# Two unused buffers shift the addresses of all large buffers of a dense two-layer kernel

## The reference

```python
# first block
h = h + 0.5 * swiglu(rms_norm(h, ffn1_norm), w_gate, w_up, w_down)        # 1024 -> 2 x 2816 -> 1024
z = rms_norm(h, mix_norm) @ w_in                                           # all projections of the mixer
y_a = dsa_attention(...)                                                   # top-128 sparse attention
y_r = group_norm_heads(retention(rq, rk, rv), ret_gn) * silu(rg)
merged = sigmoid(ga) * (y_a @ w_branch_a) + sigmoid(gb) * (y_r @ w_branch_b)
h = h + merged @ w_out
h = h + 0.5 * swiglu(rms_norm(h, ffn2_norm), ...)
h = h + sigmoid(rms_norm(h, ple_norm) @ w_ple_gate) * (p @ w_ple_proj)
x = rms_norm(h, final_norm)
# second block
x = x + gla_mixer(rms_norm_2(x, l0_norm1), ...)                            # gated linear attention
x = x + conv_ffn(rms_norm_2(x, l0_norm2), ...)                             # conv of width 3, gated MLP
return rms_norm_2(x, final_norm_2)
```

## The kernel before

| buffer | first byte | modulo 256 |
|---|---|---|
| w_raw, w_hi, w_lo (L196 to L198) | 16512, 32896, 49280 | 128 |
| h, u_hi, u_lo | 65664, 82048, 98432 | 128 |
| tmp, side, ssum, rstd, ones | 114816 to 135296 | 128 |
| consts | 136864 | 160 |
| hid_hi, hid_lo (L227) | 138432, 183488 | 192 |
| yr, gy (hi and lo) | 138432, 154816 | 192 |
| mg (hi and lo) | 171200, 187584 | 192 |
| p_hi, p_lo | 199872, 203968 | 192 |
| ya_hi, ya_lo, behind `avt` of 1152 bytes | 210240, 218432 | 64 |

## Time and profile before

### The profile page before, as it was taken

One profiled execution on the slowest core, in us unless ns is written; L12 is line 12 of the kernel. 1 busy time (PEld: TensorE's weight loads), 2 busy tenths in 40 slices (PEclk: granted clock), 3 DMA queues, 4 the chain that ended last, 5 costly groups with the idle time before them and its releaser, 6 DMA issues.

```text
span 1906.7 us, 23739 instructions
## 1 busy us (share of the span) xinstructions
PE 1859.7 (98%) x8550; PEld 1497.7 (79%) x8550; DVE 798.5 (42%) x1266; ACT 707.6 (37%) x944; POOL 909.4 (48%) x708
## 2 busy tenths in 40 slices
PE   7999999999999889999999999999999999999998
PEld 5888888876888557878888888887877888888886
DVE  5222236216666545234222222256666465455212
ACT  6443423222333453234444322245325344444221
POOL 4544445386666414444444445343443454444542
PEclk9999999999999989999999999999999999999998
DMA  4323233242322212222332333232221232233331
GB/s 160 120 89 103 91 99 100 74 142 70 127 83 72 84 34 78 95 89 93 99 99 88 101 91 98 74 123 68 67 79 65 89 99 91 96 99 96 91 99 45
DMA packets 52530, 174.55 MB, mean 92 GB/s; under 512 B 6368, under 2 KB 6752, under 8 KB 52464
## 3 DMA queue, kind: packets, MB, share of 16 engines
q1 hardware_dynamic: 52288, 173.37, 28.4%
q10 hardware_dynamic: 176, 0.30, 0.1%
HBM read 166.56 MB, written 2.10 MB: 88 GB/s over the span
## 4 chain that ended last, share of the span: by engine, by line
PE 95%; DVE 2%; ACT 2%; DMA 1%; issue 0%; SPq 0%; DVEq 0%; ACTq 0%
PE acc L1483 28%; PE acc L1485 28%; PE acc L1484 28%; PE acc L1550 2%; PE acc L1552 2%; PE acc L1551 2%; PE aux L1676 1%; PE aux L1705 1%; ACT w_hi L632 1%; PE aux L1658 1%; PE acc L1729 1%; PE acc L1813 0%; PE acc L1808 0%; DVE probs L1225 0%; PE aux L1799 0%
## 5 line engine op out<-in xcount | busy, mean ns | idle before, releaser
L551 POOL TENSOR_TENSOR w_lo<-w_raw,w_hi 128x512 fp32r<-128x512 f32 (+1 forms) x633 | 822.5, 1322 | 960.3 <-ACT w_hi L632 960.2
L1483 PE MATMUL acc<-u_hi,w_lo 128*128 128x512 f32 x1592 | 632.3, 397 | 12.3 <-POOL w_lo L551 9.8
L1485 PE MATMUL acc<-u_hi,w_hi 128*128 128x512 f32 x1592 | 623.0, 391 | 0.0
L1484 PE MATMUL acc<-u_lo,w_hi 128*128 128x512 f32 x1592 | 623.0, 391 | 0.0
L632 ACT ACTIVATE w_hi<-w_raw 128x1024 fp32r<-128x1024 f32 (+1 forms) x317 | 326.6, 1034 | 569.9 <-PE acc L1485 510.0
L1483 PEld LDWEIGHTS acc<-u_hi,w_lo 128*128 128x128 f32 x1592 | 299.7, 188 | 89.1 <-issue 19.1
L1485 PEld LDWEIGHTS acc<-u_hi,w_hi 128*128 128x128 f32 x1592 | 299.6, 188 | 65.2
L1484 PEld LDWEIGHTS acc<-u_lo,w_hi 128*128 128x128 f32 x1592 | 299.9, 188 | 63.7 <-issue 2.0
L1483 PE MATMUL acc<-hid_hi,w_lo 128*128 128x512 f32 x528 | 208.0, 394 | 0.0
L1485 PE MATMUL acc<-hid_hi,w_hi 128*128 128x512 f32 x528 | 207.0, 392 | 0.0
L1484 PE MATMUL acc<-hid_lo,w_hi 128*128 128x512 f32 x528 | 204.9, 388 | 0.0
(11 more groups left out here) (286 smaller groups left out, 1977.7 us busy)
## 6 DMA issues: line engine op xcount, KB each, us to landing
w_raw<-in_w_up SPq DMA_DIRECT2D x132, 512.0 KB, 3.5
w_raw<-in_w_mix SPq DMA_DIRECT2D x69, 512.0 KB, 3.6
w_raw<-in_w_down SPq DMA_DIRECT2D x48, 512.0 KB, 3.5
w_raw<-in_w_gla SPq DMA_DIRECT2D x32, 512.0 KB, 3.4
w_raw<-in_w_down SPq DMA_DIRECT2D x24, 384.0 KB, 3.1
w_raw<-in_w_ple SPq DMA_DIRECT2D x10, 512.0 KB, 3.5
tmp<-tmp SPq DMA_DIRECT2D x36, 64.0 KB, 2.0
h<-in_xT SPq DMA_DIRECT2D x8, 256.0 KB, 7.1
```

The lines of the kernel that those rows point to most:

```text
L551: ins = pool.tensor_tensor(w_lo[:, slot, part], w_raw[:, slot, part], w_hi[:, slot, part].bitcast(F32), ALU.subtract)
L1483: pe.matmul(o, w_lo[:, slot, columns], x_hi, start=first, stop=False)
L1484: pe.matmul(o, w_hi[:, slot, columns], x_lo, start=False, stop=False)
L1485: return pe.matmul(o, w_hi[:, slot, columns], x_hi, start=False, stop=last)
```

## The change

A buffer of 8 float32 a partition is allocated ahead of `w_raw`, and one of 2 float32 ahead of the region. Nothing reads or writes them. No other line changes.

```diff
@@ -193,6 +193,7 @@
             return ctx.enter_context(nc.semaphore(name))
 
 
+        sb("pad_ring", [P, 8])
         w_raw = sb("w_raw", [P, RING, SLAB])
         w_hi = sb("w_hi", [P, RING, SLAB], F32R)
         w_lo = sb("w_lo", [P, RING, SLAB], F32R)
@@ -222,6 +223,8 @@
         ident = consts[:, C_ID:C_ID + P]
         gain_sq, tok_root = small[:, 40:48], small[:, 24:32]
 
+
+        sb("pad_region", [P, 2])
 
         with ExitStack() as region:
             hid_hi = sb("hid_hi", [P, KF, S], F32R, region)
```

## The result

The changed kernel takes 1916.91 us (median of 4 runs, 1916.03 to 1917.93), against 1905.42 us for the kernel before (4 runs): a ratio of 1.0055, 95% interval 1.0042 to 1.0068. It is slower by some 8 to 13 us.

The account below looks back on a forecast made before the run. TensorE, busy 98% of the span, was taken to bound the kernel. The terms sum to +2.4 us, all from the region's tiles, on a median of 1905.55, giving 1908.0 us; range 1898 to 1920, meant to hold 8 in 10.

Parts of the forecast that it names:

- The bound: Whole kernel: TensorE, busy 98% of the span, bounds it; the weight path runs ahead and is held back by it.
- Where the buffers go: SBUF addresses modulo 256: ring, h and u go from 128 to 160, hid and gy from 192 to 0, ya to 128.
- Part 1: 4728 u matmuls and 768 token matmuls: operands shift by 32 together, so 0 us; u bounds -63 to +32 us.
- Rival 3: Odd 32 bytes cost in ring and u: u goes to ya's price, +32 us, 1937.7 us; chance 0.10.
- Part 2: 2208 matmuls on hid, yr, gy, mg, p: 228.9 to 230.0 ns each, +2.4 us; bounds -4.9 to +10.2.
- the straight line through the prices at 0, 64 and 192: Matmul price by distance from ring: about 2.2 ns per 64 bytes, putting distance 96 at 230.0 ns.
- Rival 2: The region's tiles go on to ya's price, 233.5 ns: +10.2 us, 1915.7 us; chance 0.24.
- Block 5 of the step avw: Counter-evidence at distance 96: two steps in 0.45 us, about 226 ns, with a stationary operand of 72 columns.
- Block 1: Same avw step, at distance 224: three steps in 0.70 us, 233 ns, in a stream that has not settled.
- five stretches at full clock: Timeline stretches said to be without waits, read for distances between matmul starts: u 226.7, hid and gy 228.9, ya 233.5 ns.
- Part 3: 96 ya matmuls: between 226.7 and 235 ns, worth -0.7 to +0.1 us; taken as 0.
- Parts 4 and 5: ScalarE, VectorE and GpSimd accesses, and loads: hidden, 0; the first loads' bare wait for x changes under 0.5 us.

## Why the prediction was right, and where not

**What it stood for.** The prediction's forecast was that no difference could be told, 1908.0 us with a range of its own of 1902 to 1909.3, and this did not come true: the kernel is 11.5 us slower, three times the 3.8 us that the prediction took as the least that can be told. The 1916.91 us lie inside its wide range of 1898 to 1920, which held a gain and a loss alike. The bounding engine, the addresses and the kind of effect were right; the price put on it was not.

**The bound.** Right: the whole loss is TensorE's own, the waits of GpSimd and ScalarE grew with it, and w_lo's wait stayed at 10 us.

**Where the buffers go.** Right: the time acts as the table of addresses says. The run with the first pad alone (0.9999) shows that moving ring and u from 128 to 160, with the region along, does nothing. With ring and region both at a multiple of 256 the ratio is 0.9966 instead of 1.0055.

**Part 1, u and token tiles at 0.** Right, 226.6 ns after the change. Rival 3, a price of the odd 32 bytes, is out.

**Part 2, the region's tiles.** The mechanism, that the price goes by the distance from the ring, was right, and the run with everything shifted together shows it. The size failed: the step was the straight line through the prices at 0, 64 and 192, which gave 230.0 ns and +2.4 us where 233.3 ns and +9.7 were measured. The line had no ground, since the curve isn't one: 32 costs as much as 96, and 64 is a low place between them. What was drawn as the likely value lay where no distance measured has its price. Rival 2, at 233.5 ns and 1915.7 us, is what happened, at 1916.9 us; it had a chance of 0.24. There were three values, two near each other and one far, and no mechanism that joined them, so the ends deserved more than the middle. The range of 1898 to 1920 held because it had taken its bounds from those ends; that is no evidence for the line.

**The sample against it.** Block 5 of the step avw spoke for 226 ns at distance 96 and was misleading, as the caution beside it said: two steps with a stationary operand of 72 columns in a stream that had not settled. The block has a third step, which was left out, from 386.46 to the next matmul at 386.70 us, 0.24; all three take 0.69 us, 230 ns each. Block 1 gave the plateau's value, which in such a stream may be chance. The prediction also speaks of five stretches at full clock; there are four, and the fifth, at 0.50, is the comparison.

**Part 3, ya.** Right, 233.5 ns before and after: 192 and 224 are both on the plateau.

**Parts 4 and 5.** Right. The start differed by 1.0 us between two profiled executions, more than the 0.5 us that I had allowed, but the piece varied without regard to addresses (6.39 to 6.81 us in the twelve profiles of the experiments, and 7.61 in the one profile before).

**The skill's rules.** The Trainium skill (Advanced Engine Details and Errata, section SBUF Cachelines) knows 16-byte lines alone, by which none of these placements differ. The runs at distances 0 and 32, both multiples of 16, are 6.6 ns apart; here the measurement decides, and that rule is not the full account. The Trainium skill (DMA: Bandwidth & Descriptors, section How a descriptor splits into AXI transactions) would save one part in nine of the rows of x with h at a multiple of 256, 0.7 us of 6.6, if it holds for the side that is written, as the prediction took it; the page speaks of where the bytes read start. The run with h there waited 6.73 us for x, amid the others' 6.39 to 6.81: no saving that a profile shows.

## What to carry to other kernels

Where TensorE bounds a float32r kernel, read the distance between matmul starts in settled stretches, for every family of operands; a family that pays more than another of the same shape points to its place in SBUF. For float32r matmuls of 512 columns at full clock, what counts here is the place of the moving operand relative to the weights, modulo 256 bytes, so give them the same place; a round address alone buys nothing. A pad of 32 bytes ahead of the region alone cost 0.5%, one of 96 bytes ahead of h and u 1.4%. For another shape measure anew. Compute the addresses that the allocator really gives, and don't interpolate a price between addresses.

## What was not expected of the hardware

- The price of a 128x512 float32r matmul depends on where its operands lie, 226.7 ns at a distance of 0 and 233.3 at 32, and only 64 lies in between (228.9); most of the distances tried are dear, 160 the dearest (234.4).
- At the lower clock the distance had no price: 426.7 ns at distance 96 and at 0.
- All three matmuls of a rotation share the price: with w_lo alone moved, u went to 232.5 ns, with hid_lo alone moved, hid to 231.0.
- Matmuls of 256 columns had it the other way: 120.0 ns at distance 0, 118.8 at 160, read in one stretch each; 120.7 and 119.3 on average over the whole traces.
